# Two expert layers of a transformer: four experts side by side in 32-column groups instead of two in 64-column groups, with 24 load buffers instead of 16

## The chip, the cores and the metric

The kernel runs on one core of a Trainium2 chip. The metric is the device time of one execution in microseconds, the median of several runs; lower is better.

## What is computed

A first block (a gated feed-forward layer, a mixer of three attention branches, a second feed-forward layer) is followed by a second block of two layers. Each of its layers has a mixer and then a mixture of experts, and this last part is what the change touches:

```python
group_probs = softmax(t @ w_rg + b_rg)             # 256 tokens, 4 groups of 8 experts
p_group, g_idx = top_k(group_probs, 1)
p_exp, e_idx = top_k(softmax(in_group), 2)         # two of the 8 experts of that group
weights = p_group * p_exp / sum(p_exp)
act = silu(t @ w_g[e]) * (t @ w_u[e])              # 1024 -> 256, 32 experts
out += (act * combine[:, e]) @ w_d[e]              # 256 -> 1024
```

All is float32. There are 256 tokens of 1024 features and 32 experts of 256 hidden features in each of the two layers. An expert gets 16 tokens on average. Counted from the reference's own choices on the inputs used here, the fullest expert gets 30 tokens in the first of the two layers and 32 in the second.

## The kernel before

**The stream of weights.** All weights lie in HBM as tiles of 128 partitions x 1024 float32 (512 KB). SyncE (SP) issues them in the order of use (`load`, line 642), each into a buffer of a ring; the load of a tile waits until the tile that last used the buffer is consumed. Outside the experts the ring has 6 buffers (`raw`), and ScalarE and VectorE split each tile into a high and a low part (`whi`, `wlo`; lines 1527 and 1974). The expert tiles aren't split: TensorE multiplies them in float32. For them the ring has 16 buffers (`RING`, line 208): 6 `raw`, 2 `over_pool`, and 8 `over_splits` that lie where `whi` and `wlo` are. The loads of the first 16 expert tiles of a layer are issued while the mixer's last products run, as those buffers come free. One layer's experts are 192 tiles, 100.7 MB.

**A layer's experts.** After the mixer's output product, VectorE works out the router's choice (lines 2602 to 2645). Meanwhile TensorE turns the tokens (line 1365), ScalarE writes their high part `hhi` (line 1901) and VectorE their low part `hlo` (line 2653, four instructions). TensorE counts each token's rank within its expert (lines 1373 to 1377), VectorE makes the slot numbers and a flag that says whether an expert has more tokens than slots (lines 2659 to 2664), and then the 0/1 matrix `select` of the first two pairs (line 2667). TensorE clears the sums in `acc` (line 975), and all four engines read the flag and branch past the overflow path (lines 729, 1384, 1909 and 2690). That path, which computes all experts for all tokens, is left out when no expert overflows.

Then `moe_events` (line 114) is an order written out by hand that TensorE, ScalarE and VectorE each walk through. An event is one of

- first, G: gather the tokens of four experts (two pairs) into `xg`: a product of the token halves with `select` (line 1417), scaled and shifted by ScalarE (line 1920) or VectorE (line 2723)
- gu: one 128-row slice of the gate and up weights, a tile for two experts. Each expert has 64 slots and its own half of the array's columns; the two matmuls write PSUM partitions 0 to 63 and 64 to 127 (line 1467)
- A: silu and product (lines 1937 and 2738); T: turn the result (lines 1480 and 1940)
- d: the down product, 4 tiles for two experts (line 1492); Y: its high and low part, weighted (lines 1950 and 2746)
- V: `select` turned, and the slots' weights (lines 1437, 1440, 1928 and 2734)
- S: scatter into `acc`, 16 matmuls (line 1503)

`turn(p)` is the stretch for pair p; there are 16 turns. It has 8 gu of pair p, 4 d of pair p-1, S of pair p-2, V, T, and two G while there is still a later set to gather (p below 14). The matmul of the pair is written so:

```python
for e in range(2):
    a = (2 * (p % 2) + e) * SLOTS
    mm = pe.matmul(work[0][SLOTS * e:SLOTS * e + SLOTS, :], xg[:, p // 2 % 2, k, a:a + SLOTS],
                   w[:, e * 512:(e + 1) * 512], start=(k == 0), stop=(k == DC - 1),
                   skip_group_check=True)
```

After the last turn VectorE adds `acc` to the residual (line 2072), ScalarE loads the table of the square root (line 1569) and squares (line 1540), and TensorE sums the squares for the next norm (line 787).

Of the kernel before, what the change touches and what calls it, by code (L numbers as in the profile page):

```python
# [17 lines left out]
F32 = mybir.dt.float32  # L18
F32R = mybir.dt.float32r
# [4 lines left out]
P = 128  # L24
# [24 lines left out]
PAIRS = EXPERTS // 2  # L49
SLOTS = P // 2  # L50
# [7 lines left out]
def columns(widths):  # L58
    out, at = {}, 0
    for name, n in widths:  # L60
# [7 lines left out]
           ("inv_count", len(WINDOWS) * 16), ("slots", 64)]  # L68
# [25 lines left out]
def moe_order():  # L94

    out = [("gu", 0, k) for k in range(8)]
    for p in range(1, PAIRS):
        out += [(what, p if what == "gu" else p - 1, k) for what, k in GU_D]
    return out + [("d", PAIRS - 1, k) for k in range(4)]

# [8 lines left out]

FOURS = PAIRS // 2  # L110
MOE_TURN = 48


def moe_events(event):


    def turn(p):
        d, scatter, gather = p >= 1, p >= 2, p // 2 + 1 < FOURS
# [37 lines left out]
    for p in range(PAIRS):  # L156
        turn(p)
    event("T", PAIRS - 1, 0)
    event("d", PAIRS - 1, 0)
    event("d", PAIRS - 1, 1)  # L160
    event("S", PAIRS - 2, 0)
    event("S", PAIRS - 2, 1)
    event("Y", PAIRS - 1, 0)
    event("S", PAIRS - 2, 2)
    event("d", PAIRS - 1, 2)
    event("d", PAIRS - 1, 3)
    event("Y", PAIRS - 1, 1)
    for j in range(3):
        event("S", PAIRS - 1, j)


G_ALL = DC + 2 * (PAIRS - 2)
G_ACT_ALL, G_DVE_ALL = DC // 2 + 2 * (PAIRS - 2), DC // 2
S_PART = ((0, 3), (3, 6), (6, 8))
CHOSEN = (0, 1, 2, 5)
S_LAST = [(PAIRS - 2, DC // 2 - 1)] + [(PAIRS - 1, m) for m in (1, 3, 5)]
# [31 lines left out]
SIDE, RING = RAW + 2, RAW + 2 + 2 * AHEAD  # L208
# [75 lines left out]
def shared(semaphore, events):  # L284
    out, at = {}, 0
    for name, count in events:
# [15 lines left out]
                            ("dn_osq", 1), ("dn_oroot", 1)])}  # L302
# [156 lines left out]
def program(nc, wstream, ada_d, c_d, consts_d, params_d, x_d, mem_d, rows_d, out_d):  # L459
    with ExitStack() as ctx:  # L460
# [114 lines left out]
        select = sb("select", [P, QT, PAIRS, P], F32R)  # L575
        selectT = sb("selectT", [P, PAIRS, T], F32R)
# [11 lines left out]
        tiles = raw + over_pool + over_splits  # L588
        ln_squares = sb("ln_squares", [P, 4, T])
        yshi = sb("yshi", [P, D], F32R)  # L590
        yslo = sb("yslo", [P, D], F32R)
        rt = sb("rt", [P, 640])
        halves = sb("halves", [P, QT, PAIRS, 4], F32R)
# [4 lines left out]

        def tile_loaded(eng, r, i=None, turn=6):
            name = f"loaded{SLOT[r]}"  # L600
            eng.wait_ge(s(name), along(after(name, 16 * USES[r]), i, 16 * (turn // (RING if of_experts(r) else RAW))))
# [17 lines left out]
        def spare_units(eng, unit):  # L619


            def pair(p, i):
                for j in range(2):
                    gu = [moe_place("gu", p, k) for k in range(8)]
                    d = [moe_place("d", p, k) for k in range(4)]
                    unit(2 * p + j, gu, d, i)
            pair(0, None)
            with eng.Fori(0, PAIRS - 2) as i:
                pair(1, i)
            pair(PAIRS - 1, None)  # L630
# [5 lines left out]
        def _(sp):  # L636
# [5 lines left out]
            def load(r, i=None):  # L642
                q = BEFORE[r]
                l = int(STREAM[r][0][-1]) if of_experts(r) else None
                if l is not None and SLOT[r] >= RAW and (q is None or q < START[f"moe{l}"]):
                    if SLOT[r] >= SIDE:
                        sp.wait_ge(s("pe_tile"), SPLITS[last_split(l, (SLOT[r] - SIDE) % AHEAD)] + 1)
                    else:
                        sp.wait_ge(s("pe_tile"), START[f"pool{l}"] + 1)
# [6 lines left out]
                sp.dma_start(tiles[SLOT[r]][:], src).then_inc(s(f"loaded{SLOT[r]}"), 16)  # L656
# [55 lines left out]
        def _(pool):  # L712
# [14 lines left out]
            for l in range(LAYERS):  # L727
                pool.wait_ge(s("flag_ready"), l + 1)
                with pool.If(pool.value_load(overflow[0:1, l:l + 1], min_val=0, max_val=1) > 0):
                    def unit(u, gu, d, i):  # L730
                        if u > 0:
                            pool.wait_ge(s(f"spare_free{l}"), along(u, i, 2))
# [3 lines left out]
                        def tile(r):  # L736
                            at = START[f"moe{l}"] + r
                            src = wstream[at:at + 1, :, half] if i is None else wstream[bass.ds(at + 12 * i, 1), :, half]
                            return src.rearrange("o p c -> (o p) c")
# [10 lines left out]
        def _(pe):  # L750
# [372 lines left out]
            def event(what, n, part=None):  # L1123
# [129 lines left out]
                elif what == "cmp_mm":  # L1253
                    pe.wait_ge(s("hidden_ready"), 2)
# [14 lines left out]
                elif what == "cmp_scores":  # L1269
                    pe.wait_ge(s("cmp_kv"), 5)  # L1270
# [22 lines left out]
                elif what == "cmp_values":  # L1293
                    pe.wait_ge(s("pct_ready"), 1)
# [23 lines left out]
            for l in range(LAYERS):  # L1318
# [64 lines left out]
                claim(range(4), "y_low", 2 * PAIRS * (l + 1))  # L1383
# [25 lines left out]
                pe.wait_ge(s("slots_ready"), 4 * l + 1)  # L1409
                base = PAIRS * l  # L1410
                tok_hi = hhi[:, :, :].rearrange("p c t -> p (c t)")
                tok_lo = hlo[:, :, :].rearrange("p c t -> p (c t)")

                def gather(bank, c, sel, at=0):
                    for j, tok in enumerate((tok_hi, tok_lo)):
                        for q in range(QT):
                            mm = pe.matmul(work[bank][:, at:at + T], tok[:, q * D + c * P:q * D + (c + 1) * P],  # L1417
                                           sel(q), start=(j + q == 0), stop=(j + q == 2), skip_group_check=True)
                    return mm

                def event(what, p, k):
                    if what == "first":
                        if k >= 4:
                            done = s("g_high") if k % 2 == 0 else s("g_copy")
                            pe.wait_ge(done, (G_ACT_ALL, G_DVE_ALL)[k % 2] * l + (k - 4) // 2 + 1)
                        gather(k % 4, k, lambda q: select[:, q, 0:2, :].rearrange("p n t -> p (n t)")
                               ).then_inc(s("g_mm"), 1)
                    elif what == "V":
                        if p == 0:
                            pe.wait_ge(s("g_copy"), G_DVE_ALL * l + DC // 2)  # L1430
                            pe.wait_ge(s("slots_ready"), 4 * l + 2)
                        else:
                            pe.wait_ge(s("act_turned"), base + p)
                        if p == 1:
                            pe.wait_ge(s("slots_ready"), 4 * (l + 1))
                        for q in range(QT):
                            pe.matmul(work[1][:, q * P:(q + 1) * P], select[:, q, p, :], identr[:],
                                      start=True, stop=True)
                        for q in range(QT):
                            mm = pe.matmul(work[1][:, T:T + 4], select[:, q, p, :], halves[:, q, p, :],  # L1440
                                           start=(q == 0), stop=(q == QT - 1))
                        mm.then_inc(s("selectT_mm"), 1)
                    elif what == "G":
                        if k == 0:
                            pe.wait_ge(s("selectT_ready"), base + p + 1)
                            pe.wait_ge(s("wslot_read"), 2 * (base + p + 1))
                        else:
                            pe.wait_ge(s("g_high"), G_ACT_ALL * l + DC // 2 + 2 * p + 1)
                        n = 2 * (p // 2 + 1)
                        for j in range(2):  # L1450
                            mm = gather(1, 4 * (p % 2) + 2 * k + j,
                                        lambda q: select[:, q, n:n + 2, :].rearrange("p n t -> p (n t)"), j * T)
                        mm.then_inc(s("g_mm"), 1)
                    elif what == "gu":
                        if p == 0 and k % 2 == 0:
                            pe.wait_ge(s("g_high"), G_ACT_ALL * l + max(k // 2 + 1, 3))
                        elif p == 0:
                            pe.wait_ge(s("g_copy"), G_DVE_ALL * l + k // 2 + 1)
                        elif k == 0 and p % 2 == 0:
                            gather_read(pe, l, p)  # L1460
                        if k == 0:
                            pe.wait_ge(s("mprod"), base + p)
                        r = moe_tile(l, "gu", p, k)
                        w, _ = tile_ready(r)
                        for e in range(2):
                            a = (2 * (p % 2) + e) * SLOTS
                            mm = pe.matmul(work[0][SLOTS * e:SLOTS * e + SLOTS, :], xg[:, p // 2 % 2, k, a:a + SLOTS],  # L1467
# [1467 lines left out]
```

## Time and profile before

| | |
|---|---|
| median of 3 runs | 1724.56 us (1724.08 to 1725.15) |
| the profiled execution | 1723.64 us |
| its span, first to last instruction | 1722.0 us |
| mean granted TensorE clock | 0.965 of full speed |
| busy share of TensorE, VectorE, ScalarE | 96%, 54%, 38% |
| read from HBM | 416.73 MB, 244 GB/s over the span |
| first layer's expert products | about 1013 to 1273 us |
| second layer's expert products | about 1450 to 1710 us |

The profile is of one execution. The span leaves out 1.64 us before the first and after the last instruction. PE is TensorE, PEld its weight loads, DVE VectorE, ACT ScalarE, SPq the queue of SyncE that issues the loads. "PEclk" and "granted clock" are shares of 2.4 GHz. "DMA share" is the mean busy share of the core's 16 DMA engines. A float32 matmul shows as two instructions in the trace, so x4 is two matmuls.

### The profile page before, as it was taken

To read this page: it belongs to the slowest core of one execution; us is meant where nothing else is said; L and a number is where in the kernel's file an instruction comes from. 1 tells how busy PE (TensorE), PEld (TensorE's weight loads), DVE (VectorE), ACT (ScalarE), POOL (GpSimd) and SP (SyncE) were. 2 spreads that over 40 slices of the span, in tenths; PEclk is the share of its full clock that TensorE was granted. 3 is DMA by queue.
4 is the path that set the end of the run, shared out by engine and by line. 5 is a ranking of instruction groups with operands and counts; after the bars stand their busy time and mean duration, and the time that the engine had idled before them with its cause. 6 is when DMAs were issued, how large, how long until landed. Compare 5 with 4: busy or idle time off the path is not lost.

```text
span 1722.0 us, 29103 instructions
## 1 busy us (share of the span) xinstructions
PE 1653.5 (96%) x11271; PEld 1323.7 (77%) x11271; DVE 935.8 (54%) x1654; ACT 647.5 (38%) x1060; POOL 3.7 (0%) x9
## 2 busy tenths in 40 slices
PE   8999999999989999999999999999999999999998
PEld 7999989899878989999898954444459896444444
DVE  6888868753454768888697641111149864111112
ACT  5544456223355544444523332222243253222222
POOL 0000000000000000000000000000000000000000
PEclk9999999899799999999899999999999999999999
DMA  8998835113333549888243669999944356999993
GB/s 329 368 361 303 285 124 184 62 37 103 130 111 123 166 156 340 308 307 298 99 147 113 223 231 394 378 389 381 382 185 150 114 188 230 395 387 377 385 384 152
DMA packets 115806, 420.96 MB, mean 244 GB/s; under 512 B 12944, under 2 KB 13088, under 8 KB 115568
## 3 DMA queue, kind: packets, MB, share of 16 engines
q1 hardware_dynamic: 114624, 414.19, 65.7%
q0 software_dynamic: 1072, 5.21, 0.8%
q8 instruction: 80, 1.31, 0.3%
q14 instruction: 30, 0.25, 0.0%
HBM read 416.73 MB, written 2.62 MB: 244 GB/s over the span
## 4 chain that ended last, share of the span: by engine, by line
PE 75%; DVE 15%; ACT 6%; issue 3%; DMA 0%; SPq 0%; DVEq 0%; ACTq 0%
PE work L827 19%; PE work L1467 13%; PE acc L827 11%; DVE yconv L2502 6%; PE work L1492 5%; PE work L919 5%; PE work L1417 4%; PE acc L1503 3%; PE work L787 2%; ACT whi L1527 2%; DVE wlo L1974 2%; PE work L862 2%; ACT xg L1920 2%; PE work L904 1%; PE work L797 1%
## 5 line engine op out<-in xcount | busy, mean ns | idle before, releaser
L1974 DVE TENSOR_TENSOR wlo<-raw,whi 128x1024 fp32r<-128x1024 f32 x264 | 321.2, 1223 | 187.5 <-ACT whi L1527 187.2
L1527 ACT ACTIVATE whi<-raw 128x1024 fp32r<-128x1024 f32 x264 | 276.9, 1056 | 281.5 <-PE work L827 186.3
L827 PE MATMUL work<-hhi,whi 128*128 128x256 f32 x1024 | 291.8, 285 | 2.9 <-DVE hlo L2002 1.3
L827 PE MATMUL work<-hlo,whi 128*128 128x256 f32 x1024 | 290.1, 283 | 0.0
L827 PE MATMUL work<-hhi,wlo 128*128 128x256 f32 x1024 | 290.0, 283 | 0.0
L827 PEld LDWEIGHTS work<-hhi,whi 128*128 128x128 f32 x1024 | 196.7, 192 | 5.5 <-DVE wlo L1974 2.8
L827 PEld LDWEIGHTS work<-hlo,whi 128*128 128x128 f32 x1024 | 196.8, 192 | 0.1
L827 PEld LDWEIGHTS work<-hhi,wlo 128*128 128x128 f32 x1024 | 196.7, 192 | 0.0
L2738 DVE TENSOR_TENSOR pair_b<-work,pair_a 128x256 f32<-128x256 f32 x32 | 13.6, 425 | 304.2 <-ACT pair_a L1937 304.2
L1920 ACT ACTIVATE xg<-work,mod,gscale 128x256 f32<-128x256 f32 x120 | 61.7, 561 | 222.1 <-PE work L1417 222.1
L1467 PE MATMUL work<-over_splits,xg 128*64 128x512 f32 x480 | 120.8, 607 | 2.3 <-DVE pair_b L2738 1.8
L2080 DVE SCALAR_TENSOR_TENSOR ada_tiles<-ada_tiles,c_act 128x1024 f32<-128x1024 f32 x96 | 116.2, 1218 | 1.9 <-DMA ada_tiles<-ada_d 1.9
L862 PE MATMUL work<-hf,raw 128*128 128x256 f32 x512 | 113.2, 383 | 0.0
L862 PEld LDWEIGHTS work<-hf,raw 128*128 128x128 f32 x512 | 98.7, 193 | 13.9
L1467 PE MATMUL work<-raw,xg 128*64 128x512 f32 x408 | 101.7, 606 | 3.0 <-DVE pair_b L2738 2.3
L827 PE MATMUL acc<-ahi,whi 128*128 128x256 f32 x352 | 99.5, 283 | 2.9 <-DVE alo L2115 2.9
L919 PE MATMUL work<-hhi,whi 128*128 128x256 f32 x288 | 86.7, 301 | 15.2 <-ACT gates L1535 10.7
L2502 DVE SCALAR_TENSOR_TENSOR yconv<-vpad,params,yconv 128x256 f32<-128x256 f32 x240 | 99.4, 478 | 1.4
L827 PE MATMUL acc<-alo,whi 128*128 128x256 f32 x352 | 98.9, 281 | 0.0
L827 PE MATMUL acc<-ahi,wlo 128*128 128x256 f32 x352 | 98.7, 280 | 0.0
L919 PE MATMUL work<-hlo,whi 128*128 128x256 f32 x288 | 84.8, 294 | 0.0
L919 PE MATMUL work<-hhi,wlo 128*128 128x256 f32 x288 | 83.7, 291 | 0.0
(426 smaller groups left out, 2978.1 us busy)
## 6 DMA issues: line engine op xcount, KB each, us to landing
raw<-wstream_d SPq DMA_DIRECT2D x448, 512.0 KB, 4.8
over_splits<-wstream_d SPq DMA_DIRECT2D x192, 512.0 KB, 6.0
ada_tiles<-ada_d SPq DMA_DIRECT2D x96, 512.0 KB, 5.2
over_pool<-wstream_d SPq DMA_DIRECT2D x48, 512.0 KB, 6.1
bias_rows_d<-rt POOLq DMA_DIRECT2D x1, 1536.0 KB, 11.3
xT<-x_d SPq DMA_DIRECT2D x4, 256.0 KB, 3.7
mem_in<-mem_d POOLq DMA_DIRECT2D x1, 1024.0 KB, 5.4
tb<-bias_rows_d POOLq DMA_DIRECT2D x1, 1024.0 KB, 7.0
```

The lines of the kernel that those rows point to most:

```text
L827: mm = pe.matmul(out, a, b, start=(start and k == 0), stop=(stop and k == n - 1), skip_group_check=skip)
L862: mm = pe.matmul(work[bank][:, 0:T], h[:, c * P:(c + 1) * P], hf[:, c, :], start=(c == 0), stop=(c == DC - 1))
L919: mm = pe.matmul(bank[:, 0:T], ((h, h, l)[k % 3])[:, c * P:(c + 1) * P], ((hhi, hlo, hhi)[k % 3])[:, c, :], start=(k == 0), stop=(k == 23))
L1417: mm = pe.matmul(work[bank][:, at:at + T], tok[:, q * D + c * P:q * D + (c + 1) * P], sel(q), start=(j + q == 0), stop=(j + q == 2), skip_ ...
L1467: mm = pe.matmul(work[0][SLOTS * e:SLOTS * e + SLOTS, :], xg[:, p // 2 % 2, k, a:a + SLOTS], w[:, e * 512:(e + 1) * 512], start=(k == 0), ...
L1492: mm = pe.matmul(work[2 + half][own, :], turned[:, f, own], w[:, e * 512:(e + 1) * 512], start=(f == 0), stop=(f == 1), skip_group_check=True)
L1503: mm = pe.matmul(acc_c[:, m, :], y[:, m * P:(m + 1) * P], sel, start=False, stop=False, skip_group_check=True)
L1527: act.activation(whi[n % AHEAD][:], tiles[SLOT[SPLITS[n]]][:], ACT.Copy).then_inc(s("hi_done"), 1)
L1920: return act.activation(out, src, ACT.Identity, bias=mod[:, b:b + 1], scale=gscale[:, g:g + 1])
L1974: dve.tensor_tensor(wlo[n % AHEAD][:], tiles[SLOT[SPLITS[n]]][:], whi[n % AHEAD][:].bitcast(F32), ALU.subtract).then_inc(s("lo_done"), 1)
L2080: dve.scalar_tensor_tensor(ada_tiles[:, k, :], ada_tiles[:, k, :], 1.0, c_act[:], ALU.mult, ALU.mult, accum_out=out).then_inc(s("ada_done" ...
L2502: ins = dve.scalar_tensor_tensor(yconv[:, c, :], vpad[:, c, i:i + T], w, yconv[:, c, :], ALU.mult, ALU.add)
```

## The change

Four experts are handled at once. The 16 pairs become 8 quads (`QUADS`), an expert has 32 slots instead of 64, and its matmuls use 32 columns of the array and 32 partitions of PSUM. A gu or d event of a quad consumes two tiles, so a turn consumes 24 tiles instead of 12, and there are 8 turns instead of 16 with the same events in each; `select`, `selectT` and `halves` shrink by half. The ring gets 8 more buffers (`EXTRA`): four in the room that `select` gives up, two in `spare_d`, and `yconv` and `ln_squares`. Two neighbours of these share a semaphore, so each waits for both. The overflow check and its path move behind the last turn on every engine, `acc` is cleared in turn 1, and three of the four low parts of the tokens are written after the first `select`; TensorE multiplies four high parts before it waits for low parts. Some semaphores of the mixer are merged, with the counts adjusted. The diff, cut to its core:

```diff
-PAIRS = EXPERTS // 2
-SLOTS = P // 2
+QUADS = EXPERTS // 4
+SLOTS = P // 4
...
-SIDE, RING = RAW + 2, RAW + 2 + 2 * AHEAD
+SIDE = RAW + 2
+EXTRA = SIDE + 2 * AHEAD
+RING = EXTRA + 8
...
-    out = [(first + j) % RAW for j in range(RAW)] + list(range(RAW, SIDE))
+    out = [(first + j) % RAW for j in range(RAW)] + list(range(RAW, SIDE)) + list(range(EXTRA, RING))
...
-                    if SLOT[r] >= SIDE:
+                    if SLOT[r] >= EXTRA:
+                        sp.wait_ge(s("pe_tile"), START[f"conv{l}"] + 4)
+                    elif SLOT[r] >= SIDE:
...
-                claim(["acc"], "x_ready", 4 * (5 + 2 * l))
-                clear([acc[:, b * 512:(b + 1) * 512] for b in range(4)])
+                claim(range(4), "y_low", 2 * QUADS * (l + 1))
+                pe.wait_ge(s("slots_ready"), 4 * l + 1)
...
+                pe.wait_ge(s("ht_high"), 4 * l + 3)
+                for c in range(4):
+                    gather(c, c, first, 0, (0,))
...
+                        if k < 4:
+                            pe.wait_ge(s("ht_low"), 4 * l + 2)
+                            gather(k, k, first, 0, (1,)).then_inc(s("g_mm"), 1)
+                            return
...
+                        r = moe_tile(l, "gu", p, 2 * k)
+                        for e in range(4):
+                            if e % 2 == 0:
+                                w, _ = tile_ready(r + e // 2)
+                            a = (4 * (p % 2) + e) * SLOTS
+                            mm = pe.matmul(work[0][SLOTS * e:SLOTS * e + SLOTS, :], xg[:, p // 2 % 2, k, a:a + SLOTS],
+                                           w[:, e % 2 * 512:(e % 2 + 1) * 512], start=(k == 0), stop=(k == DC - 1),
+                                           skip_group_check=True)
+                            if e % 2 == 1:
+                                mm.then_inc(s("pe_tile"), 1)
...
-                for b in range(4):
+                def low_tokens(b):
                     dve.wait_ge(s("ht_high"), 4 * l + b + 1)
...
+                low_tokens(0)
...
                 ins.then_inc(s("slots_ready"), 1)
+                for b in (2, 1, 3):
+                    low_tokens(b)
...
                 moe_events(event)
+                act.wait_ge(s("flag_ready"), l + 1)
+                with act.If(act.value_load(overflow[0:1, l:l + 1], min_val=0, max_val=1) > 0):
```

## Rows read from the trace of the kernel before

**Rows 1.** Windows; columns: us, busy us of each engine (instructions), granted clock, DMA share, GB/s

```profile
1000.00:1010.00 10.00, 7.71 (x39) 4.95 (x38) 8.50 (x39) 4.38 (x7) 0.00 (x0) 0.88 0.01 3
...
1099.00:1132.00 33.00, 32.63 (x174) 15.30 (x172) 4.29 (x10) 8.71 (x18) 0.00 (x0) 1.00 1.00 384
```

**Rows 2.** Waits of the SP queue, 1010 to 1265 us: us in total, times, longest us

```profile
SPq L656 <- PE work L1467: 138.7, 116, 19.8
```

**Rows 3.** Chain that ended last, whole span: start us, us, what

```profile
934.35 14.63 PE work L862 x64
...
1059.07 1.97 PE acc L1503 x16
...
1092.01 1.97 PE acc L1503 x16
```

**Rows 4.** The same chain, late turns of the first layer

```profile
1238.12 1.87 PE work L1467 x8
1239.98 0.37 PE work L1437 x2
1240.35 0.17 PE work L1440 x2
...
1243.51 1.72 PE work L1492 x8
...
1251.54 0.37 PE work L1480 x2
```

**Rows 5.** The same chain, gather in the first turns

```profile
1030.81 1.14 PE work L1417 x8
```

**Rows 6.** DMA view, 1470 to 1485 us, second layer, early turns

```profile
DMA packets 1692, 6.17 MB, mean 411 GB/s; under 512 B 187, under 2 KB 187, under 8 KB 1692
```

**Rows 7.** DMA view, 1250 to 1262 us, last loads of the first layer

```profile
DMA packets 1365, 4.96 MB, mean 413 GB/s; under 512 B 154, under 2 KB 154, under 8 KB 1365
```

**Rows 8.** DMA view, 1050 to 1250 us, first layer

```profile
DMA packets 20944, 76.39 MB, mean 382 GB/s; under 512 B 2325, under 2 KB 2325, under 8 KB 20933
```

**Rows 9.** Timeline of the SP queue: start us, us, what

```profile
981.35 0.91 SPq L656 DMA_DIRECT2D over_pool<-wstream_d  x2
982.30 11.99 SPq L656 DMA_DIRECT2D over_splits<-wstream_d  x8
1014.46 6.65 SPq L656 DMA_DIRECT2D raw<-wstream_d  x6
```

**Rows 10.** DMA view, 984 to 998 us, loads ahead of the first layer

```profile
DMA packets 1543, 5.64 MB, mean 403 GB/s; under 512 B 168, under 2 KB 168, under 8 KB 1542
```

**Rows 11.** Chain, start of the first layer's experts

```profile
1003.12 2.64 DVE hlo L2653 x4
...
1006.48 0.68 DVE select L2667 x2
1007.16 0.66 issue
1007.82 5.45 PE work L1417 x32
1013.26 3.58 PE work L1467 x16
```

**Rows 12.** Chain, end of the first layer's experts

```profile
1268.39 1.89 PE work L1492 x8
...
1270.30 0.03 ACT yshi L1950
...
1275.06 5.01 PE work L787 x32
```

**Rows 13.** Timeline, VectorE's flag and ScalarE after it

```profile
1006.34 0.14 DVE L2664 CAST overflow<-rt 1x1 int32<-1x1 f32 x1
...
1007.44 1.28 ACT L1920 ACT_TABLE_LOAD   x1 [4.87 <-DVE overflow L2664]
```

**Rows 14.** Windows, same columns, at the first gathers

```profile
1006.50:1010.50 4.00, 3.05 (x14) 2.69 (x13) 2.51 (x13) 1.85 (x2) 0.00 (x0) 0.63 0.03 6
```

More of the change, by code:

```diff
@@ L94, in moe_order, with both @@
 def moe_order():
[L96 to L99, printed above, removed]
+    def both(what, p, k):
+        return [(what, p, 2 * k + h) for h in range(2)]
+    out = [t for k in range(8) for t in both("gu", 0, k)]
+    for p in range(1, QUADS):
+        for what, k in GU_D:
+            out += both(what, p if what == "gu" else p - 1, k)
+    return out + [t for k in range(4) for t in both("d", QUADS - 1, k)]
 MOE_ORDER = {t: n for n, t in enumerate(moe_order())}
@@ L574, in program @@
         xg = sb("xg", [P, 2, DC, T])
-        select = sb("select", [P, QT, PAIRS, P], F32R)
-        selectT = sb("selectT", [P, PAIRS, T], F32R)
+        select = sb("select", [P, QT, QUADS, P], F32R)
+        selectT = sb("selectT", [P, QUADS, T], F32R)
+        over_select = [sb(f"over_select{i}", [P, TILE]) for i in range(4)]
         vpad = sb("vpad", [P, 4, 30 + T])
@@ L596, in program, with landed @@
         overflow = sb("overflow", [1, LAYERS], mybir.dt.int32)
+        def landed(slot):
+            return f"loaded{slot}" if slot < EXTRA else f"loaded_both{(slot - EXTRA) // 2}"
         def tile_loaded(eng, r, i=None, turn=6):
-            name = f"loaded{SLOT[r]}"
-            eng.wait_ge(s(name), along(after(name, 16 * USES[r]), i, 16 * (turn // (RING if of_experts(r) else RAW))))
+            name = landed(SLOT[r])
+            each = 16 if SLOT[r] < EXTRA else 32
+            eng.wait_ge(s(name), along(after(name, each * USES[r]), i, each * (turn // (RING if of_experts(r) else RAW))))
         EVAC = {}
@@ L619, in spare_units, with quad @@
         def spare_units(eng, unit):
[L622 to L630, printed above, removed]
+            def quad(p, i):
+                for j in range(4):
+                    gu = [moe_place("gu", p, 2 * k + j // 2) for k in range(8)]
+                    d = [moe_place("d", p, 2 * k + j // 2) for k in range(4)]
+                    unit(4 * p + j, gu, d, i)
+            quad(0, None)
+            with eng.Fori(0, QUADS - 2) as i:
+                quad(1, i)
+            quad(QUADS - 1, None)
         block = ctx.enter_context(nc.Block())
@@ new lines, in gather, with first @@
+                def gather(bank, c, sel, at=0, parts=(0, 1)):
+                    for j in parts:
+                        tok = (tok_hi, tok_lo)[j]
+                        for q in range(QT):
+                            mm = pe.matmul(work[bank][:, at:at + T], tok[:, q * D + c * P:q * D + (c + 1) * P],
+                                           sel(q), start=(j + q == 0), stop=(j + q == 2), skip_group_check=True)
+                    return mm
+                def first(q):
+                    return select[:, q, 0:2, :].rearrange("p n t -> p (n t)")
```

369 lines of the change are left out of this document (180 added, 189 removed).

## The prediction

> **What bounds the kernel now.** I read the windows of the expert stage first. In steady state, in the stretch of two turns, [rows 1] TensorE is busy 32.63 of 33.00 us at full clock, VectorE and ScalarE 4.3 and 8.7 us. The same row has the 16 DMA engines busy all the time, at 384 GB/s. Two resources look full, so which one sets the pace? The waits of the SP queue say it: of the 255 us of the first layer's experts it spent 138.7 us waiting for a product to free a buffer [rows 2], and the chain runs from TensorE instruction to TensorE instruction without a DMA in it [rows 3 to 5]. TensorE sets the pace: 33.0 us for two turns (from the scatter at 1059.07 to the one at 1092.01, two turns later) [rows 3], which is 24 tiles or four experts.
>
> Is the DMA near its own limit? Whenever TensorE had freed several buffers at once, the loads ran at 411 and 413 GB/s for 15 and 12 us [rows 6, 7]; over the 200 us in between they ran at 382 [rows 8], the pace at which buffers came free. A tile of 524,288 bytes takes 1.276 us at 411 and 1.372 us at 382. So 24 tiles take 30.6 us at the higher rate, and TensorE's 33.0 us are only 2.4 us above that. **The next bound stands close behind the present one.**
>
> **TensorE's work per four experts.** A gu tile with its two experts takes 0.935 us in a run of two (1.87 for x8) and 0.86 us in a longer one, a d tile 0.86 (1.72 for x8) [rows 4]. I take 0.86. That two groups really run side by side is seen from the mixer: there 32 float32 matmuls of 256 columns take 14.63 us, 0.457 us each [rows 3], so one of 512 columns would take 0.91 us alone, and here two take 0.86. The rest of a turn is V 0.54, T 0.37, S 1.97 and two gathers of 1.14 [rows 3 to 5], 5.2 us. Check: 12 x 0.86 + 5.2 = 15.5 of the 16.5 us per turn, 1.0 us of gaps.
>
> After the change a turn has the same events for twice the experts. If four groups run side by side, it takes the same 16.5 us for four experts. If only two do, the 24 tiles take 20.6 us and the turn 26.8. No row shows four; these are the ends. Both lie below the 30.6 us of the 24 loads, so it doesn't matter to the sum: either way **TensorE waits for weights**. When tiles come one by one the real case is near the second end, since the second pair of experts can't start before its own tile.
>
> **Where it becomes the loads' pace.** Before the first product all 24 buffers should be full. The loads ahead of the stage are issued from 981.35 us [rows 9] at 403 GB/s [rows 10]; after the 16 tiles of today the DMA stands still until 1014.46 (its share is 0.01 from 1000 to 1010) [rows 1, 9]. Eight more tiles are 10.2 us and fit in that hole. Their buffers are free from the mixer's fourth convolution tile on, before the 8 split buffers behind them in SP's order, so this wait holds up nothing. The shared semaphore delays every first tile of these neighbours by one tile's time, 1.28 us, at most four times per 24 tiles; TensorE needs the neighbour at once anyway, so I cost it at nothing.
>
> **The start.** Today's order is VectorE's four low parts 2.64 us, select 0.68, 0.66 us of reading the flag, gathers 5.45, first product at 1013.26 [rows 11]. Three low parts (2.0 us) and the 0.66 go behind or away, and so does TensorE's clearing of `acc` (it moves into turn 1, four matmuls of some 0.25 us, hidden by the loads later on). But VectorE then still has the three low parts and the weights' small operations ahead of its first copy of a gather, and TensorE waits for that copy. I take 1.2 us of the 2.7 (bounds: nothing, and 3.5 if the short wait also spares the half clock that the first gathers have now, 0.63 granted [rows 14]). First product at 1012.0, first load 1.2 us later as today [rows 9, 11], 1013.2.
>
> **The sum for one layer.** 192 - 24 = 168 tiles come after that. First arrival after about 2 us (estimate: with several in flight the page has 4.8 us from issue to landing, and a tile behind another adds 1.28). 168 x 1.276 = 214.4. Last tile at 1013.2 + 2.0 + 214.4 = 1229.6; its matmuls 0.9, so the last down product ends at 1230.5. Today it ends at 1268.39 + 1.89 = 1270.28 [rows 12]. Difference -39.8 us. Behind it everything is as now (Y, the last S, the table, squares; 4.8 us to the sums [rows 12]), except that each engine reads the flag there. From the flag's write to ScalarE's next instruction it is 1.0 us today (1006.48 to 1007.44) [rows 13]; at the end ScalarE is on the chain, so +0.9 (bounds 0.3 and 2). The next stage's six raw tiles now queue behind the last expert tile and land within 7.7 us of it, the first two within 2.6; ScalarE splits those some 4 us after it (2.2 us and the 0.9 behind the last down product). Hidden; without that cover it would be 1 to 3 us. Layer total -38.9. The second layer has the same turns and nearly the same length (1450 to 1710 us in the table), so -77.8 together.
>
> The profiled execution took 1723.64 us: 1723.64 - 77.8 = 1645.8. It lies 0.9 us under the median of the runs shown, so I say **1647**. Nothing else changes: the merged semaphores count the same events, the smaller `select` is written in the same number of instructions, and the four slot-weight reductions of V instead of two add 2 x 0.17 us on VectorE, which is idle 87% of the stage [rows 1].
>
> The Trainium skill, page HBM Reference, Specifications and the text under it, gives about 358 GB/s per core when the other core of the domain streams too and about 425 for one alone. By 358 the 168 tiles would take 246.0 us and the result would be near 1710; by 425 207.2 us and 1632. The trace of this case has 411 and 413, near the figure for one core alone, and decides.
>
> **The rivals.**
>
> *The loads don't go faster than now* (0.13). For it: a DMA share of 1.00 at 384 GB/s. Against: 411 and 413 GB/s in [rows 6, 7], where several buffers were free at once. Then 168 x 1.372 = 230.5, 16.1 us more per layer: 1679. Values between are as likely, and the range takes them in.
>
> *TensorE's clock falls while it waits for tiles* (0.12). For it: after its wait at 1007 us the first gathers were granted 0.63 of full speed [rows 14]. Against: it would wait under half a microsecond at a time, every tile giving it 0.86 us of work in 1.28, and once it lagged at 1.2 GHz, tiles would pile up, the groups would run four at once, and it would be busy all the time. At 1.2 GHz throughout, four at once, a turn takes 2 x 16.4 = 32.8 us, today's pace, and only the end gains: about 1718. Half of the turns so: about 1683. [...]
>
> *The four groups exclude each other* (0.04), the case that ends slower. Where: the gu and d matmuls. Price: with each group at 0.86 us the 12 sets of four take 41.3 us, the turn 47.4 instead of 33.0, x 16 turns = +230: about 1954. It decides from 2.24 us per set of four on ((33.0 - 6.1) / 12). Against: two groups run side by side in 0.86.
>
> *The change doesn't do what it says* (0.01): an expert has more than 32 tokens and the path for all tokens runs, 48 matmuls of 256 columns for each of 32 experts, 48 x 32 x 0.457 = 702 us for a layer: about 2350. The fullest has 32, and the flag asks for more than 32.
>
> **How the numbers follow.** The forecast keeps 0.70. Its own range is 1638 (420 GB/s and the better start) to 1660 (400 GB/s and 2 us lost at each end). To hold 8 in 10, I reach up over the first rival and half of the second: 1638 to 1684. A measurement of this kernel can tell about 0.2% from no change. All of the forecast, the first rival and nearly all of the second are faster by more: 0.94; within 0.2%: 0.01; slower: 0.05.
>
> **What would show it.** Right: first-layer products from 1012 to 1231 us; DMA at 405 to 415 GB/s in a whole stretch of 200 us; TensorE waiting for DMA from the second or third turn on, turns of 30 to 31 us; SP's wait for products nearly gone; the DMA idle for under 7 us ahead of the stage; clock 1.00. Wrong: a rate near 382 with full buffers outstanding (first rival); a clock well under 1 in the stage (second); turns over 33 us with TensorE busy (third); an end that grew by more than 2 us between the last down product and the squares.

## The result, and the profile after

The changed kernel takes 1659.77 us (median of 4 runs, 1656.90 to 1663.58), the kernel before took 1724.68 beside it (1724.08 to 1725.15): a ratio of 0.9619 (0.9606 to 0.9632), 64.9 us less. Forecast were 77.8 less and 1647 us. The direction, the cause and the range held; the size was 13 us off.

| | before | after |
|---|---|---|
| the profiled execution, its span | 1723.64, 1722.0 us | 1658.83, 1657.2 us |
| mean granted clock | 0.965 | 0.946 |
| busy share of TensorE, VectorE, ScalarE | 96%, 54%, 38% | 92%, 55%, 35% |
| first layer's expert products | 1013.3 to 1270.3 us | 1014.9 to 1237.1 us |

Windows of the kernel after, with the columns of [rows 1]: just ahead of the experts, their start, and three stretches of steady state.

```profile
1000.00:1010.00 10.00, 8.23 (x53) 5.99 (x52) 8.44 (x40) 4.59 (x9) 0.00 (x0) 0.95 0.99 397
1010.00:1033.00 23.00, 21.57 (x163) 10.18 (x166) 7.02 (x26) 6.33 (x12) 0.00 (x0) 0.88 0.67 254
1033.00:1066.00 33.00, 27.64 (x170) 9.17 (x162) 2.55 (x7) 5.48 (x11) 0.00 (x0) 1.00 1.03 410
1099.00:1132.00 33.00, 27.55 (x149) 9.54 (x142) 2.55 (x7) 4.46 (x9) 0.00 (x0) 0.92 1.03 409
1198.00:1231.00 33.00, 25.80 (x130) 5.94 (x128) 3.05 (x8) 2.69 (x6) 0.00 (x0) 0.90 1.03 409
```

Against [rows 1] the stretch 1099 to 1132 has 27.55 us of TensorE instead of 32.63, and 409 GB/s instead of 384. TensorE has gaps; the DMA engines have none (share 1.03). Ahead of the stage, where they stood still (3 GB/s), they now bring eight more tiles (397 GB/s). The hole has moved to 1010 to 1033, where all 24 buffers are full and none is free yet (254 GB/s).

Waits of the kernel after, 1010 to 1240 us: those of TensorE's queue for tiles, then those of the SP queue (columns as in [rows 2]).

```profile
PEld work L1469 <- DMA over_splits<-wstream_d: 41.0, 42, 1.4
...
PEld work L1496 <- DMA raw<-wstream_d: 17.3, 18, 1.1
```

```profile
SPq L669 <- PE work L1469: 21.4, 3, 18.7
```

SP's 138.7 us of waiting [rows 2] are 21.4, of which 18.7 are the one wait before the first buffer comes free. TensorE waits for single tiles instead, about 1 us at a time. The DMA view of the kernel after, 1030 to 1230 us, answers to [rows 8], and a long timeline row of its SP queue to [rows 9]:

```profile
DMA packets 22459, 81.86 MB, mean 409 GB/s; under 512 B 2497, under 2 KB 2497, under 8 KB 22451
```

```profile
983.58 2.48 SPq L669 DMA_DIRECT2D over_select<-wstream_d  x4
...
1016.55 3.31 SPq L669 DMA_DIRECT2D raw<-wstream_d  x6
...
1037.60 7.34 SPq L669 DMA_DIRECT2D raw<-wstream_d  x6
...
1068.63 7.36 SPq L669 DMA_DIRECT2D raw<-wstream_d  x6
```

409 GB/s is 1.282 us for a tile of 524,288 bytes, and 24 of them are 30.8 us. From one use of the `raw` buffers to the next it is 31.0 us (1037.60 to 1068.63): the turn for four experts goes at the loads' pace. The start and the end are in the chain of waits of the kernel after, here first the start:

```profile
1006.61 0.67 DVE select L2700 x2
1007.28 1.98 DVE hlo L2685 x3
1009.26 0.08 DVE rt L2712
...
1011.21 0.24 DVE rt L2722
...
1011.47 0.55 DVE xg L2729
...
1012.07 2.93 PE work L1404 x12
1014.99 3.95 PE work L1469 x32
```

After `select` the chain stays on VectorE for 4.7 us: three low parts (1.98), the small operations for the weights (2.2 us, from L2712 at 1009.26 to L2722), and only then its first copy of a gather (0.55), for which TensorE waits. Before, the gathers began 0.66 us after `select` [rows 11]. They begin early now too, with the high parts; it is their last twelve instructions (2.93 us) that stand behind the copy. The same chain at the end of the first and of the second layer:

```profile
1220.50 15.50 DMA over_splits<-wstream_d
...
1236.05 1.08 PE work L1496 x4
...
1242.14 4.88 PE work L802 x32
...
1638.61 1.08 PE work L1496 x4
...
1642.99 6.24 PE work L802 x32
```

The chain at the end of a layer is a load, its matmuls, and what follows. The last sums of squares take 6.24 us.

For all that follows I read five instants per layer from the trace: the first low part that VectorE writes, the first gu product, the first load issued after it, the end of the last down product, and the start of the sums of squares. The differences, in us, each from one profiled execution (first and second layer, where they differ):

| | before | after |
|---|---|---|
| low part to first product (start) | 10.15, 10.06 | 10.60 |
| first product to last down product (stage) | 257.06, 256.97 | 222.18, 222.05 |
| last down product to sums of squares | 4.81, 3.11 | 5.04, 3.33 |
| last sums of squares to the end of the kernel | 11.92 | 14.12 |

### The profile page after: what moved, and what is told of

Read it like the earlier page. It is cut to its first block, busy times and chain, and to the rows that moved or that the text cites. A ratio compares the mean times of both kernels' runs of the same rounds, so it can differ in the third digit from the quotient of the medians.

```text
span 1657.2 us, 27505 instructions
## 1 busy us (share of the span) xinstructions
PE 1517.8 (92%) x10663; PEld 1210.9 (73%) x10663; DVE 904.3 (55%) x1606; ACT 576.6 (35%) x914; POOL 3.7 (0%) x9
## 4 chain that ended last, share of the span: by engine, by line
PE 55%; DVE 14%; DMA 12%; SPq 11%; issue 4%; ACT 4%; DVEq 0%; ACTq 0%
PE work L842 20%; PE acc L842 11%; SPq L669 10%; DMA over_select<-wstream_d 7%; DVE yconv L2534 6%; PE work L934 5%; DMA over_splits<-wstream_d 5%; PE work L802 2%; PE work L1469 2%; ACT whi L1559 2%; PE work L877 2%; DVE wlo L2006 2%; PE work L812 2%; PE work L919 1%; PE work L785 1%
## 5 line engine op out<-in xcount | busy, mean ns | idle before, releaser
L2744 DVE TENSOR_TENSOR pair_b<-work,pair_a 128x256 f32<-128x256 f32 x16 | 6.8, 424 | 235.4 <-ACT pair_a L1961 235.4
L1469 PE MATMUL work<-over_splits,xg 128*32 128x512 f32 x448 | 108.6, 603 | 18.2 <-DMA over_splits<-wstream_d 16.3
L1469 PEld LDWEIGHTS work<-over_splits,xg 128*32 128x32 f32 x448 | 16.0, 108 | 99.4 <-DMA over_splits<-wstream_d 82.2
L1944 ACT ACTIVATE xg<-work,mod,gscale 128x256 f32<-128x256 f32 x56 | 29.0, 560 | 163.3 <-PE work L1404 163.3
```

The source lines that it names most:

```text
L1944: return act.activation(out, src, ACT.Identity, bias=mod[:, b:b + 1], scale=gscale[:, g:g + 1])
```

## The experiments

Each was made from the changed kernel. Times are medians; ratios are to the kernel before, timed beside it on the same chip (1725.55, 1726.86 and 1725.86 us in the three groups of four versions). The second group, from the half loads to the start with the first slice, has no control of its own; its ratios are held against those of the controls in the other two. Start, stage and end are read from one profiled execution of each version.

**The changed kernel again**, as a control.

> The changed kernel, unaltered, beside the others. The loads set the pace: about 1659 us, the turns 30.7 us, expert stage (first product to last down product) 222 us per layer. If instead TensorE with its clock at 0.92 set it, the times of the single runs would follow the granted clock of the stage; by the theory of the loads they don't.

Measured: 1657.66 us (5 runs, 1652.13 to 1664.45), ratio 0.9615 (0.9590 to 0.9640). Start, stage and both ends agree with the first profile within 0.2 us. Single runs scatter by 12 us, though; where this comes from stands in the last section.

**16 buffers instead of 24**, four groups kept.

```diff
-RING = EXTRA + 8
+RING = EXTRA
...
-    out = ... + list(range(RAW, SIDE)) + list(range(EXTRA, RING))
+    out = ... + list(range(RAW, SIDE))
```

> Four experts at once, but a ring of 16 buffers: 176 instead of 168 tiles come after the stage has begun. If the loads set the pace, each layer loses 8 x 1.28 = 10.3 us: 1659.8 + 20.5 = 1680, and the pace inside stays at 409 GB/s. If TensorE sets the pace, the buffers only matter for its waits and it stays within 5 us of 1660. Against the kernel before that leaves 44 us to the grouping and 20 to the buffers.

Measured: 1679.11 us (4 runs), ratio 0.9735 (0.9708 to 0.9762). The stage takes 232.29 and 232.64 us, 10.1 and 10.6 more. Eight tiles more after the first product are 8 x 1.282 = 10.3. Windows of this kernel:

```profile
1099.00:1132.00 33.00, 29.45 (x148) 8.48 (x144) 2.54 (x7) 4.46 (x9) 0.00 (x0) 1.00 1.03 409
```

The rate is 409 GB/s with 16 buffers too. So the number of buffers doesn't make the loads faster; more buffers make fewer of them fall after the first product. Of the 68 us between the kernel before and the control, the change with its old 16 buffers is worth 46 and the eight buffers another 21. Two groups with 24 buffers weren't run, so it isn't shown what the buffers are worth by themselves, nor how much of the 46 the groups alone bring. That each tile fewer is worth its own transfer time is what only a stage bound by loads shows.

**All four low parts ahead of the choice**, as before the change.

```diff
-                low_tokens(0)
+                for b in range(4):
+                    low_tokens(b)
...
                 ins.then_inc(s("slots_ready"), 1)
-                for b in (2, 1, 3):
-                    low_tokens(b)
```

> The four low parts of the tokens are all written ahead of the ranks and the select, as in the kernel before; all else as changed. My theory: the first products wait for VectorE's first copy of a gather, which comes behind the same sum of VectorE's work in either order, so the first product stays where it is (8.4 us after the select now, about 7.1 us after a select that comes 1.3 us later): 0 us, at most 1 per layer. The rival, the reasoning of the prediction, has the select on the path: 1.2 us more per layer, 2.5 in all.

Measured: 1658.46 us (5 runs), ratio 0.9616 (0.9597 to 0.9635), not told apart from the control. In the trace the start takes 9.85 and 9.70 us, 0.75 and 0.90 less than with the low parts behind. Its chain:

```profile
1005.69 2.64 DVE hlo L2685 x4
...
1008.90 0.14 DVE overflow L2698
1009.04 0.68 DVE select L2701 x2
...
1009.96 5.56 PE work L1404 x32
```

While VectorE writes the four low parts (2.64 us), TensorE computes the ranks; after them the flag and then `select` follow within 0.72 us. In the changed kernel one low part is ahead and VectorE then waits for the ranks. Moving the low parts behind the choice bought nothing that can be measured. How much of the 0.75 and 0.90 us the order itself costs isn't shown, since the clock differs along with it: from the start of `select` to the first product TensorE was granted 0.73 here and 0.64 in the changed kernel. The section on the prediction comes back to this.

**The small operations of the weights later** (into the first event that uses them), low parts as in the changed kernel.

```diff
-                dve.wait_ge(s("router_exp"), 2 * l + 2)
-                ...
+                def shares():
+                    dve.wait_ge(s("router_exp"), 2 * l + 2)
+                    ...
...
+                        if k == 0:
+                            shares()
```

> VectorE's small operations for the slots' weights (2.2 us) move behind its four copies of the first gathers. If VectorE's queue ahead of its first copy is what delays the first product, that comes 2 us sooner per layer, and so does everything behind it, since the loads restart with it: -4 us, 1656. If the half clock of TensorE or the gathers themselves set it: 0 us.

Measured: 1655.72 us (5 runs), ratio 0.9597 (0.9577 to 0.9616); the interval overlaps the control's. The trace shows the start shorter by 1.9 and 3.1 us (8.72 and 7.47). Here too the clock takes part: from `select` to the first product it was 0.73 in the first layer and 1.00 in the second, against 0.64 with the small operations in their old place. So VectorE's queue ahead of its first copy delays the first product, but by less than these two numbers say.

**Half loads.** The tiles after the first 24 are loaded only in their left 512 columns; the rest of the buffer keeps what it had, so half of the weights are left out.

```diff
-                sp.dma_start(tiles[SLOT[r]][:], src)
+                cut = slice(0, TILE // 2 if l is not None and i is not None else TILE)
+                sp.dma_start(tiles[SLOT[r]][:, cut], src[:, cut])
```

> After a layer's first 24 expert tiles, every load brings only the left 512 of 1024 columns, half the bytes; the right half keeps what was there, so part of the expert weights is wrong. It shows TensorE's own pace with four groups. If the four groups run side by side (0.99 us per set of four, as in the first turn), a turn is 12 x 0.99 + 5.2 + 1 = 18 us, near the 15.4 us that half the bytes take, and the stage falls from 222 to 145 us or less per layer: about 1505. If only two run at a time, a turn is 26.8 us and the stage some 200: about 1610. If the stage isn't bound by the loads at all: 1659.

Measured: 1468.07 us, a single run. The stage takes 126.54 and 126.77 us. A window and the chain of this kernel:

```profile
1070.00:1100.00 30.00, 29.54 (x245) 13.37 (x248) 4.92 (x14) 8.72 (x18) 0.00 (x0) 1.00 1.05 387
```

```profile
1060.06 1.92 PE work L1470 x16
...
1067.73 1.72 PE work L1497 x16
...
1076.63 1.92 PE work L1470 x16
```

Here TensorE is the bound: it is busy 29.54 of 30 us, and from 1040 to 1140 us it waits for no load, although the DMA share is 1.05 as well. Its turn is 16.57 us (1060.06 to 1076.63). Sixteen instructions are two sets of four gu products in 1.92 us, 0.96 each; the down products take 0.86 per set. Four groups of 32 columns run side by side as two of 64 did [rows 4]. That settles the rival in which they exclude each other, and leaves TensorE 14.2 us of slack in each 30.8 us turn.

**More products on TensorE**: V's two matmuls six times over, about 1.9 us a turn.

```diff
-                        for q in range(QT):
+                        for q in [0, 1] * 6:
```

> The two matmuls that turn the select in V run six times instead of once, 10 more per turn, each some 0.18 us: TensorE gets 1.9 us more to do per turn, 15 us per layer. If the loads set the pace this is hidden but for the last turns: within 2 us of 1658. If TensorE, waiting at a granted clock of 0.92, sets it: +25 to +30.

Measured: 1659.14 us (4 runs), ratio 0.9603 (0.9583 to 0.9622); stage 222.24 and 222.82 us, 0.1 and 0.8 more than in the first profile. Sixteen turns with 1.9 us each would be 30 us if TensorE set the pace. They are hidden.

**A warm end**: three products of zeros behind each of the last turn's first three down events, and four more of the norm's own fillers.

```diff
+                        if p == QUADS - 1 and k < 3:
+                            for _ in range(3):
+                                pe.matmul(work[1][:, :], zero[:, :], ...)
...
-            norm_sum(7 + 3 * LAYERS)
+            norm_sum(7 + 3 * LAYERS, (4, 0, 0, 0))
```

> Three more products of zeros behind each of the last turn's down products but one, and four ahead of the last norm's sums. In the profiles of the changed kernel the last norm runs at half the clock (14.1 us from the first sum to the end, before 11.9). If that comes from TensorE's waits for the last tiles, this brings back up to 2.2 us; if from the wait for the squares alone, four products fill only 0.9 us of it and it stays within 1 us. The fillers themselves fall into waits for tiles and cost under 0.5 us.

Measured: 1655.77 us (5 runs), ratio 0.9596 (0.9578 to 0.9614), overlapping the control's. In the trace the part behind the last sums' start takes 11.51 us instead of 14.12. A chain row and a window of this kernel, and under them the window of the changed kernel at the same work:

```profile
1641.85 3.48 PE work L802 x32
```

```profile
1640.00:1646.00 6.00, 5.45 (x45) 4.86 (x43) 3.14 (x9) 3.15 (x7) 0.00 (x0) 0.93 0.01 4
```

```profile
1642.50:1649.50 7.00, 6.22 (x32) 6.17 (x32) 2.03 (x6) 2.49 (x5) 0.00 (x0) 0.59 0.01 4
```

The sums take 3.48 us in the one and 6.24 in the other; the windows around them were granted 0.93 and 0.59. So the longer end goes with the clock. That the products of zeros bring the clock back isn't shown: the changed kernel without them had the fast end too in its third profile, the control further down. And they have a price. The stage is 222.63 and 223.03 us here, 0.6 and 1.1 more than in the control of the first group, and the last sums begin 3.63 us after the last down product instead of 3.33.

**Start with the first slice.** The second half of the gathers moves between the first gu products, and the small operations of the weights into the first event that uses them.

```diff
+        if p == 0:
+            event("first", 0, 4)
         event("gu", p, 1)
+        if p == 0:
+            event("first", 0, 5)
...
+            event("first", 0, 7)
+            event("rest", 0, 0)
         event("V", p, 0)
...
-    for c in range(DC):
+    for c in range(4):
         event("first", 0, c)
-    event("rest", 0, 0)
...
-                        gather(k % 4, k, first).then_inc(s("g_mm"), 1)
+                        gather(1 + k % 3, k, first).then_inc(s("g_mm"), 1)
```

> The first gate and up product of a layer starts after four gathered slices instead of eight (the other four stand between the first products), and VectorE's small operations for the slots' weights come later, as in the third experiment. If the stage is bound by the loads from its first to its last tile, whatever brings the first product forward brings the end forward by as much, since the first freed buffer restarts the loads: first product 3.5 us after the select instead of 8.4, so -9 to -10 us over two layers, 1649. If TensorE's work in the first turns sets it, the total work is the same and it stays near the third experiment's 1656.

Measured: 1655.67 us (5 runs), ratio 0.9590 (0.9575 to 0.9605), a miss of 6 us and an interval that overlaps those of both controls. The start is 4.4 us shorter (6.21 instead of 10.60; up to 1.2 of it can be the clock, as the section on the prediction shows), but the stage 2.9 and 2.2 longer (225.12, 224.22). Its chain:

```profile
1018.72 0.68 PE work L1411 x4
...
1019.42 0.54 DVE xg L2738
1019.97 0.08 DVE rt L2721
...
1022.16 0.77 DVE select L2708 x2
...
1023.07 0.41 PE work L1446 x2
```

V needs the small operations and the second `select`, and both now stand behind VectorE's last copy: TensorE waits from 1019.4 to 1023.1. Buffers come free that much later: no load is issued between 1019.5 and 1025.4 us, and when the next goes out, only two of those before it haven't landed. Windows of this kernel, with the rate last:

```profile
1024.00:1030.00 6.00, 6.00 (x41) 2.51 (x33) 2.05 (x8) 2.38 (x4) 0.00 (x0) 0.73 0.93 341
1030.00:1036.00 6.00, 6.00 (x50) 2.46 (x47) 0.42 (x1) 1.79 (x4) 0.00 (x0) 1.00 0.93 341
```

The loads run at 341 GB/s for 12 us. In a stage bound by loads, a wait of TensorE costs if it holds back a buffer until the loads have nearly run out, and at the start they do.

**The changed kernel once more**, beside the last three.

> The changed kernel, unaltered, once more as a control for this chip: 1656 to 1660 us, 222 us from the first product to the last down product in each layer.

Measured: 1660.29 us (5 runs), ratio 0.9619 (0.9603 to 0.9635). The starts (10.60 us) and stages (222.43 and 222.09) are those of the first profile, but the end isn't: from the last sums on it takes 11.6 us instead of 14.1, without any product of zeros. The row of its chain, and under it that of the kernel before:

```profile
1648.40 3.72 PE work L802 x32
```

```profile
1710.00 3.72 PE work L787 x32
```

The granted clock was 1.00 in these 3.7 us. So one and the same kernel ends fast in one execution and slowly in another.

**The start mended**: the small operations directly behind VectorE's copy of slice 3, ahead of its later copies.

```diff
                                           ALU.mult, ALU.add).then_inc(s("g_copy"), 1)
+                        if k == 3:
+                            shares()
                     elif what == "rest":
-                        if k == 0:
-                            shares()
```

> As the seventh experiment, but VectorE's small operations stand behind its second copy instead of behind the fourth. In the seventh they delayed V of turn 0 by 4.3 us, TensorE freed no buffer meanwhile, and the loads fell to 250 to 350 GB/s until about 20 us into the stage. If that is why an earlier first product brought nothing, the loads now run at 410 from the first freed buffers on and the layer ends 3 us sooner than in the seventh, select to last down product 226 us (230.6 in the changed kernel): 1649 to 1651. If the early stage is bound by something else, it stays at 1655.

Measured: 1649.47 us (5 runs, 1644.68 to 1653.56), ratio 0.9553 (0.9537 to 0.9568): faster than the control with intervals apart, 10.8 us by the medians. The start takes 6.21 us and the stage 222.82 and 222.25. Start and stage together are 229.03 and 228.46, against the control's 233.03 and 232.69, so these two make 8.2 us of the 10.8; the rest is within the scatter. The next load after the first eight goes out at 1024.35, when four haven't landed yet. The window that showed 341 in the version above:

```profile
1024.00:1030.00 6.00, 5.61 (x49) 2.87 (x49) 2.21 (x8) 3.04 (x5) 0.00 (x0) 1.00 1.03 419
```

**Start mended and the warm end.**

> The ninth with the sixth's fillers in the last turn and ahead of the last norm. In the sixth the last norm took 11.5 us where the changed kernel takes 14.1. Together: 1647 to 1649.

Measured: 1648.85 us (5 runs, 1647.14 to 1655.55), ratio 0.9570 (0.9551 to 0.9588). The end is 11.52 us instead of 13.40, but the stages are 0.4 and 1.1 us longer (223.26 and 223.32) and the last sums begin 0.3 us later, which takes nearly all of it back. The time isn't told apart from that of the version above.

**And a warm start**: seven products of zeros while TensorE waits for `select`.

> The tenth with seven products of zeros (1.5 us) between the rank products and the wait for the select, where TensorE stands still for 1.8 us and is then granted half the clock for the first gathers. If the clock there comes from that wait, the first product comes 1 us sooner per layer and with it the end: 2 us less than the tenth. If the wait is too short to matter, 0; the fillers end before the select does, so they cost under 0.3 us.

Measured: 1651.04 us (5 runs), ratio 0.9573 (0.9560 to 0.9588); the 2 us that were hoped for didn't come. The gathers run at full clock: a window from this kernel, and under it the same work in the version with the mended start.

```profile
1007.00:1011.00 4.00, 3.82 (x27) 2.66 (x28) 3.38 (x7) 1.04 (x2) 0.00 (x0) 1.00 0.80 315
```

```profile
1010.00:1014.00 4.00, 3.35 (x20) 2.69 (x24) 3.07 (x7) 1.13 (x2) 0.00 (x0) 0.75 0.79 312
```

Yet the start is only 0.2 us shorter. The first load goes out 1.24 us after the first product instead of 2.06, and still start and stage together take 229.41 us against 229.47. So the time at which the very first buffer is freed isn't what sets the end there; which later one does, wasn't tried.

## Why the prediction was right, and where it was off

**What bounds the kernel.** Right. Loads run at 409 GB/s for 200 us and turns take 31 us; with 16 buffers the stage grows by the transfer time of eight tiles, with more products it grows by under 1 us, and with half the loads it falls to 127 us.

**TensorE's work.** The turn of 16.57 us (half loads) is the lower of the two ends (16.5), when tiles are there. When they come one by one TensorE is busy for 27.55 of 33 us, 25.7 per turn of 30.8, near the other end (26.8), as the prediction said, and this costs nothing.

**The rate.** 411 was taken, 409 measured: 168 x (1.282 - 1.276) = 1.0 us per layer. The first rival (382) is refuted. The Trainium skill, page HBM Reference, Specifications, gives about 358 GB/s for a core beside another and about 425 for one alone. The measured 409 lies between, nearer to the second.

**The stage, 3.7 us too long per layer.** First product to last down product: forecast 1.2 + 2.0 + 214.4 + 0.9 = 218.5, measured 222.2. The sum of the measured terms is 1.63 until the first load, 4.05 of filling, 168 x 1.282 = 215.4, and 1.1 for the last tile. The largest error is the **fill: 2.0 us was taken for the first arrival, and it took 4.05** (from the first load at 1016.55 to the last landing at 1236.00 are 219.45 us; less 215.4). These windows of the changed kernel show it, the rate last:

```profile
1016.50:1018.50 2.00, 2.00 (x24) 0.48 (x16) 1.08 (x4) 0.00 (x0) 0.00 (x0) 1.00 0.46 113
1018.50:1020.50 2.00, 1.98 (x20) 0.68 (x12) 0.43 (x3) 0.38 (x1) 0.00 (x0) 1.00 0.93 367
1020.50:1022.50 2.00, 1.63 (x16) 1.23 (x20) 0.19 (x2) 0.41 (x1) 0.00 (x0) 1.00 0.84 231
1022.50:1026.50 4.00, 4.00 (x40) 1.75 (x36) 0.42 (x1) 2.83 (x6) 0.00 (x0) 1.00 1.03 415
```

The first transfers go slowly (113 GB/s), and there is a second dip (231) from 1020.5 on. Full rate holds only from 1022.5, 6 us after the first load. Buffers aren't short meanwhile: seven loads had been issued by 1020.2 us, and the first landed at 1020.30, the second at 1021.72. So the 4.05 us are 2.5 ahead of the first tile's own 1.28 (issued at 1016.55, landed after 3.75) and 1.6 lost in the dip. The term of the sum that failed is "first arrival after about 2 us": the first tile took half a microsecond more, and the dip wasn't in it. The kernel before shows the dip after its own restart as well (250 GB/s from 1018 to 1019), so the change didn't bring it; what makes it stays open.

**The start, 1.7 us too long per layer.** I took 1.2 us off; measured are 0.45 and 0.54 more than before. This lies outside the bound "nothing" that I gave. The prediction named VectorE's queue ahead of its first copy and didn't add it up: 1.98 of low parts and 2.2 of small operations stand between `select` and the copy, so that the gathers, which ran from 0.66 us after `select` before, can't end earlier than 0.55 us and some matmuls behind them. The other part is the clock. The half clock wasn't spared but lasted longer: from `select` to the first product TensorE was granted 0.75 before and is granted 0.64 now, and the twelve gather instructions behind the copy run at half clock. The second layer of the version with the warm end, whose start is that of the changed kernel, happened to be granted 0.76 there. The row of the changed kernel's second layer, and under it that one's:

```profile
1414.76 2.93 PE work L1404 x12
```

```profile
1413.40 1.70 PE work L1404 x12
```

Its start took 9.37 us, 1.2 less than 10.60 and 0.7 less than before the change. So without the longer half clock the new order would have gained 0.7 us, still short of the 1.2 in the sum. The version with all four low parts first took 9.85 and 9.70 at 0.73, so by this one comparison its advantage over the changed kernel was the clock's and not the order's. Which order brings which clock is seen in these profiles only as a tendency, and why stays open.

**The end.** The flag's reading was priced at 0.9 us per layer and cost 0.23 and 0.22: 1.35 us better for both. The 1.0 us that I read at [rows 13] holds more than the reading of the flag; what else, no run separates. Not in the sum at all: the last sums of squares at 0.59 of full speed, +2.2 us in the profiled execution. They came in the first two profiles of the changed kernel (6.24 and 6.16 us) and not in the third (3.72), so this term belongs to the execution that was profiled and not to the change by itself.

**The clock rival.** The prediction expected a clock of 1.00 throughout. The clock did fall in the stage, to 0.90 to 0.92 in some stretches, and stayed at 1.00 in others, and the time didn't follow, because TensorE has slack. The Trainium skill, page TensorE: Matmul & The Clock Gate, section on HAM oscillation, tells of a clock that fell in waits for DMA of 3 to 5 us. The waits here are about 1 us each, so its case isn't this one; the clock fell all the same in parts of the stage, and the 1683 or 1718 us worked out for this rival didn't come.

**The account**, both layers, against the forecast: stage +7.2, start +3.5, last norm +2.2, first block +1.3 (the first low part at 1004.32 instead of 1003.04), the flag -1.35, and 0.1 between the layers: the 13.0 between 77.8 and 64.8 (1723.64 to 1658.83 in the two profiled executions).

## What to carry to other kernels

When a change hands the bound to the loads, the time is the number of loads after the first free buffer times the time of one, plus the filling: here that took 4 us and not the latency of one transfer. Look for the first waits of the consumer: one that let the loads run down to two outstanding cost 2 to 3 us per layer, one that left four outstanding cost nothing that could be seen. Work that is moved behind a decision must be added up on the engine that it is moved to, up to that engine's next instruction that others wait for; and before it is moved, ask what wait it covers now. A start or an end of a few microseconds depends on the clock that this execution was granted: take a second profile of the same kernel before you put such a difference down to an edit.

## What the runs showed of the hardware that was not expected

- **Four column groups at the price of two.** Four float32 products in 32 columns each take 0.86 to 0.96 us together, for 512 columns of moving data, as two in 64 columns do (0.86).
- **The first block scatters.** In the control of the last group the first layer's low parts begin at 1009.41 us, with the start mended and a warm end at 1001.48, although no instruction of the first block differs. The changed kernel alone has 1004.32, 1002.68 and 1009.41 in its three profiles. Windows of the two kernels, the control first; clock is third from last:

```profile
200.00:400.00 200.00, 188.60 (x1438) 183.88 (x1438) 138.27 (x227) 88.54 (x133) 0.00 (x0) 0.94 0.35 116
400.00:600.00 200.00, 186.13 (x1501) 178.23 (x1500) 94.09 (x105) 93.04 (x190) 0.91 (x1) 0.91 0.37 123
```

```profile
200.00:400.00 200.00, 187.32 (x1462) 182.44 (x1461) 137.13 (x225) 88.91 (x135) 0.00 (x0) 0.97 0.34 115
400.00:600.00 200.00, 186.15 (x1534) 177.74 (x1534) 101.55 (x114) 94.94 (x190) 0.91 (x1) 0.94 0.39 130
```

The granted clock differs by 0.03 in both stretches, where TensorE is busy 93 to 94% of the time. That goes with the 8 us; why it does so in some executions stays open. The kernel before scatters as well: in the three groups its nine runs each span 5 to 6 us, those of the two controls 12 and 6. It is why effects of 2 to 4 us had to be read from the traces' stretches rather than from the medians.
